# Joint attention stage: the query groups of a head in the order 0, 1, 3, 2

## The reference

```
s = einsum('bqhd,bkhd->bhqk', qb, k) * scale
s = s + cb[..., None] - c[:, :, None, :]
s = where(key_pos[None, :] <= q_pos[:, None], s, -inf)
p = softmax(s, axis=-1)
return einsum('bhqk,bkhd->bqhd', p, v)
```

## Time and profile before

| | us |
|---|---|
| median of 3 runs (lowest to highest) | 3654.77 (3650.62 to 3657.84) |
| the profiled execution | 3655.24 |
| its span, first to last instruction | 3653.5 |
| attention stage, first to last score | 747.4 |

### The profile page before, as it was taken

How to read it: one execution, slowest core, us unless ns; L and a number is a source line. 1 busy time by engine, 2 the same in 40 slices (tenths; PEclk the granted TensorE clock), 3 DMA queues, 4 the chain that set the end, 5 groups by cost and what they waited for, 6 DMA issues and landing times. The chain is left out here.

```text
span 3653.5 us, 48316 instructions
## 1 busy us (share of the span) xinstructions
PE 3245.6 (89%) x18078; PEld 2856.5 (78%) x18078; DVE 2103.9 (58%) x3533; ACT 837.4 (23%) x1492; POOL 491.5 (13%) x277
## 2 busy tenths in 40 slices
PE   5999999828988899956998799999998799999996
PEld 5999999715555555534676799999998699999995
DVE  5001112266666666623433587787786678778776
ACT  5111111213333333312222211111112211111112
POOL 0000000031111111000000422222223122222220
PEclk9999999858988999978999899999999899999997
DMA  4223222133221322163343311111112411111112
GB/s 110 70 70 105 64 61 61 31 88 81 64 62 47 81 56 73 30 203 113 104 137 121 111 46 46 46 46 46 46 46 84 120 46 46 46 46 46 46 46 82
DMA packets 250600, 262.36 MB, mean 72 GB/s; under 512 B 38074, under 2 KB 207435, under 8 KB 244515
## 3 DMA queue, kind: packets, MB, share of 16 engines
q1 hardware_dynamic: 249163, 256.81, 24.5%
q10 hardware_dynamic: 1344, 4.36, 0.6%
HBM read 192.08 MB, written 69.05 MB: 71 GB/s over the span
## 5 line engine op out<-in xcount | busy, mean ns | idle before, releaser
L2155 PE MATMUL ps_ffn<-h,wsp_n 128*128 128x312 f32 (+1 forms) x6336 | 1054.3, 322 | 44.0 <-POOL h L1991 29.9
L2155 PEld LDWEIGHTS ps_ffn<-h,wsp_n 128*128 128x128 f32 x6336 | 1015.1, 189 | 50.3 <-issue 38.8
L2090 DVE TENSOR_TENSOR yacc<-ps_ffn,yacc 128x312 f32<-128x312 f32 (+1 forms) x1056 | 495.1, 515 | 220.5 <-PE ps_ffn L2170 220.5
L391 PE MATMUL ps_project<-hT,wsp 128*128 128x416 f32 x3000 | 579.3, 353 | 3.2 <-DVE wsp L335 3.2
L391 PEld LDWEIGHTS ps_project<-hT,wsp 128*128 128x128 f32 x3000 | 561.3, 188 | 12.0 <-issue 4.9
L2170 PE MATMUL ps_ffn<-aT,dsp 128*128 128x312 f32 (+1 forms) x3168 | 544.9, 321 | 9.8 <-DVE yacc L2090 9.8
L2170 PEld LDWEIGHTS ps_ffn<-aT,dsp 128*128 128x128 f32 x3168 | 508.4, 188 | 12.6 <-issue 9.8
L1986 POOL TENSOR_TENSOR wsp_n<-wraw_n,wsp_n 128x1024 fp32r<-128x1024 f32 x88 | 210.5, 2392 | 801.8 <-ACT wsp_n L2027 801.8
L2104 DVE RECIPROCAL silu<-silu 128x416 f32<-128x416 f32 x132 | 306.2, 2320 | 4.5
L1012 PE MATMUL ps_fox<-pexp,va 128*65 128x512 f32 (+3 forms) x640 | 298.1, 548 | 4.7 <-ACT pexp L1155 4.7
L2057 ACT ACTIVATE aT<-a 128x416 fp32r<-128x416 f32 x132 | 65.2, 494 | 1005.5 <-DVE a L2112 1005.5
(11 more groups left out here) (235 smaller groups left out, 3062.3 us busy)
## 6 DMA issues: line engine op xcount, KB each, us to landing
wraw_n<-in_w_gate_dram SPq DMA_DIRECT2D x44, 512.0 KB, 3.9
wraw_n<-in_w_up_dram SPq DMA_DIRECT2D x44, 512.0 KB, 3.8
draw<-in_w_down_dram SPq DMA_DIRECT2D x44, 512.0 KB, 3.6
qk_raw<-zT SPq DMA_DIRECT2D x32, 512.0 KB
zT<-zs SPq DMA_DIRECT2D x12, 1040.0 KB
wraw<-in_w_in_dram SPq DMA_DIRECT2D x24, 512.0 KB
x<-x2s SPq DMA_DIRECT2D x20, 416.0 KB
h2T<-hT_m SPq DMA_DIRECT2D x20, 416.0 KB
```

The source lines that it names most:

```text
L391: last = pe.matmul(ps[:, g, 0:BLK], wsp[:, b, s, k, :], hT[:, g * TPB:(g + 1) * TPB, v, k, :], start=m == 0, stop=m == 3 * KD - 1)
L2090: dve.tensor_tensor(y, ps[:, 4 + i, 0:FB[b] * TT], y, ALU.add).then_inc(added, 1)
L2155: last = pe.matmul(ps[:, 2 * q + s, 0:FB[b] * TT], wsp[:, par, s, w, k, :], h2[:, FB0[b]:FB0[b + 1], v, k, :], start=m == 0, stop=m == 3 * ...
```

## The change

The order of the groups within each head goes from 0, 1, 2, 3 to 0, 1, 3, 2. Everything that counts by `group(u)`, `blocks(u)` and `runs(u)` follows it.

```
-GORDER = (0, 1, 2, 3)
+GORDER = (0, 1, 3, 2)
```

## The result

| | before | after |
|---|---|---|
| median of 20 runs each, us | 3657.45 (3650.62 to 3663.12) | 3663.47 (3659.57 to 3674.63) |
| profiled execution, us | 3655.24 | 3661.24 |
| attention stage, first score to its last instruction, us | 755.9 | 759.9 |

The ratio is 1.0023 [1.0015, 1.0031]: slower, by 6.0 us between the medians, where 1.7 us faster was forecast. The time lies inside the stated range of 3640 to 3664, near its edge and on the other side of no change. The two profiled executions are 6.0 us apart as well: 4.0 in the attention stage, and 2.0 in the stages around it, which the change doesn't touch (the feed-forward stage alone, first to last instruction, takes between 1645.7 and 1649.8 us in the profiles of this study, in either order). So the 4.0 are to be explained.

What follows compares the result with a forecast made beforehand. Attention stage: TensorE busy 667.2 of 747.4 us, idle mostly waiting for VectorE's maxima. Terms +11.5 - 10.7 - 2.5 = -1.7 us on 3654.8 gave 3653.1 us; own range 3645 to 3660, 8-in-10 range 3640 to 3664.

Steps and rivals of the forecast that it cites:

- ScalarE's copies and GpSimd's work keep their blocks: First units of heads 2 and 3: their long stops, up to 8.1 us, stay; listed under what costs nothing.
- term A: Group 1's units: a fourth maximum in 32 blocks adds 0.36 us wait each, 11.5 us slower; bounds 0 and 19.
- term B: Engine collisions in the two-a-block units of heads 2 to 5: of 21.7 us, 10.7 go; bounds 3 and 18.
- term C: Quiet two-a-block units of heads 1, 6 and 7: 2.5 us of TensorE idle time go; bounds 0 and 4.
- rival 2: Collisions only move: 3 us go in term B, none in term C; +8.5, 3663 us; chance 0.13.
- rival 3: Group 1's units: four maxima a block drop the granted clock to 1.2 GHz; +18, 3673 us; chance 0.09.
- waits for an exp: TensorE waiting for the exp behind ScalarE's copies: 4.7 us grows, so 7.6 us stay in term B.
- the stuck VectorE: Heads 2 to 5: TensorE waits 0 to 1.70 us each for VectorE's late reductions; 0.5 taken, so 2 us stay.
- The half clock: Lowered granted clock in the units of heads 2 to 5: 1.4 us stay; bounds 0 and 8.6.
- The sign that was named for rival 2: Group 3's units over 34 us in heads 2 to 5 would show the forecast wrong.
- head 0, which the sum left out with a remark: Head 0's unit may have another part of the idle time; noted only with the upper bound 4 of term C.
- SyncE's later load: Load of the head after next issued at block 28, not 24; costs nothing, covered by GpSimd's 261.4 us wait.

Runs made afterwards that it cites:

- experiment 1: Changed order plus one wait: GpSimd's cast L944 for the head after head 4 lets VectorE's last query factor finish first; 3658.85 us, ratio 1.0009.
- Experiment 3: Order before, with one maximum moved a block later (last of head 3's four for head 4, block 34 not 33); 3658.84 us, ratio 1.0005.
- experiment 2: Order before plus one wait holding GpSimd's cast L944 at the start of head 4 until VectorE's end factors are done; 3658.81 us, ratio 1.0003.
- experiment 7: The changed order measured again, nothing else altered; 3664.09 us, ratio 1.0016.
- experiments 5: Changed order plus waits holding GpSimd's L944 in five heads and L949 in four until VectorE's end factors are done; 3632.99 us, ratio 0.9944.
- 6: Order before plus waits holding GpSimd's L944 in five heads and L949 in four until VectorE's end factors are done; 3628.66 us, ratio 0.9916.
- experiment 9: Order before, GpSimd's L944 and L949 held for VectorE's end factors, plus two waits for negations at L947 and L949; 3615.09 us, ratio 0.9885.
- 10: Kernel of experiment 9 with group 1's 12 maxima spread over five blocks (3, 2, 3, 2, 2) instead of four; 3606.43 us, ratio 0.9858.

## Why the prediction was wrong

**The step that failed** is the one priced at nothing: "ScalarE's copies and GpSimd's work keep their blocks". GpSimd did keep its place, but VectorE did not keep its own. The last maximum of the head now stands one block later, VectorE came to the last query factor some 0.4 us later after the head's last score (0.71 us after that score's mask L1002 began, before 0.33), and a race won by 0.06 us was lost. This cost 2.0 us at head 3's end and up to 4.3 in head 4's first unit in the profile (2.7 of them went in experiment 1), and 4.6 us of the median by experiment 1. Without it no difference between the two orders can be told (1.0009 and 1.0003): where the forecast stood, but for 1.7 us that cannot be told from none either. Experiment 3 showed that the place of one maximum is enough; that this same shift is what loses the race in the changed order is argued from the two timelines.

The lost race is not the whole of the miss. Between the forecast of -1.7 and the profile's +4.0 lie 5.7 us: -1.9 from term A, +2.1 from term B (the 2.0 at head 3's end), +3.7 from term C, whose sign was wrong, and +1.8 in group 0's units, which the sum left at nothing. Those 1.8 are head 4's +4.3 and head 3's -2.4, and the latter is not the order's doing: in experiment 2, which is the kernel before up to that point, head 3's unit took 20.0 us, and in the profile before 23.1. The measured 3663.5 us is also the number of rival 2, by chance: that rival let only 3 us go in term B, and 8.6 went.

**Term A, +11.5: the mechanism and the price were right, and shown in six of the eight heads.** The fourth maximum waits 0.36 us, in 24 blocks of heads 2 to 7. In heads 0 and 1 the units grew by 1.4 and 1.5 only (in the second profile of the changed order, of experiment 7, by 6.7 and 0.3, so these two settle nothing): in head 0 TensorE stood before too, 2.25 and 2.99 us, for a VectorE that was itself held, and in head 1 the clock is low in both (0.78 in the earlier trace rows, 0.80 after). 9.6 in all. Nothing of rival 3 came: the granted clock of group 1's units in heads 2 to 7 is 1.00.

**Term B, -10.7: right in the sum, and spoilt by the failed step.** -8.6 was measured, and the 2.0 at head 3's end are the new collision; without them it is -10.6. Two of its parts were near: 8.4 us of waits for an exp over six times (7.6 forecast), 6.4 of them in heads 2 to 5, and one wait of 1.7 for the stuck VectorE (2). The forecast had put all four waits for an exp into heads 2 to 5; one of them, 0.64 us, stood in head 0, and head 5 had none. The half clock was mis-sized: all four units are at 0.95, which by the forecast's own measure is up to 0.05 x 139.6 = 7.0 us, where 1.4 were taken. That the sum came out near all the same is in part luck. The sign that was named for rival 2, units over 34 us, was drawn too tight: all four are over 34 (34.5 to 35.5), but 31.4 + 11.0 / 4 is already 34.2.

**Term C, -2.5: wrong sign, +1.2.** Heads 1 and 6 gave 1.1 and 0.6, head 7 lost 0.6, and head 0, which the sum left out with a remark, lost 2.3: its exp behind the copies came 0.7 us later (1.34 in place of 0.64), and a wait of 1.32 us for the laid maxima stood at the end of group 3's unit, where none had been. The copies stand in every head from 0 to 6; I had priced them only where they were long.

**SyncE's later load** cost nothing, as said: GpSimd waits for the last score, 249.0 us, and the one wait for a load, 41.3 us for head 1, is there in both.

**What stays open.** Head 0's unit of group 1 differs between runs of one kernel: 28.1 and 33.4 us in two profiles of the changed order, 26.7 and 30.4 in those of the order before and of experiment 3, which touches only head 4's maxima. GpSimd starts there when a load lands. How much of the medians' 6.0 against the profiles' 4.0 comes from it was not measured. The profile of experiment 7 has 762.9 us for the stage, 7.0 over before, and 6.7 of them are this unit; group 3's unit of head 2 takes 33.0 there and 34.6 in the first. So a table by units from one execution each is good to a few microseconds, and the experiments carry more than it does.

## What to carry to other kernels

When two engines race for a port, an edit that touches neither of them can flip the race: for every such pair in the trace, write down by how much it is won, and price those won by less than the edit shifts. A wait that settles the race for good is nearly free where the engine held back has slack (GpSimd waits 249 us here), and such waits were worth 43 us, against the 4 to 6 that the reordering moved; but each also shifts what comes later, and can bring the next pair together. And count each collision away before an ordering is judged: by itself this order costs 15.7 us, of which 11.7 were hidden because it happened to spare others.

## What was not expected of the hardware

- A VectorE instruction of four numbers a partition was held as long as a large one: L1239, `TENSOR_SCALAR` on 128x4, took 3.69, 3.75, 3.80 and 4.21 us beside GpSimd's 4.5 us subtraction. It takes 0.17 in most places (all 32 in the profile before), and 0.39 to 2.87 in a few others of experiments 5, 6, 9 and 10. The same page and section of the Trainium skill counts this operation among those that can take the shared ports; the trace agrees. Reductions from PSUM are not held: the 36 of L1232 that lie wholly inside a large instruction of GpSimd in the trace before take 0.69 us at most, as do the 280 elsewhere. In experiment 1 the first pair below runs ahead of a subtraction, the second mostly beside it; only their widths differ:
```profile
1226.50 0.89 DVE L1234 TENSOR_REDUCE tops<-ps_fox 128x1 f32<-128x512 f32 x2
...
1227.78 1.02 DVE L1234 TENSOR_REDUCE tops<-ps_fox 128x1 f32<-128x512 f32 x2 [0.40 <-PE ps_fox L972]
1227.91 4.51 POOL L949 TENSOR_TENSOR k_lo_rows<-qk_raw,k_hi_rows 64x2048 fp32r<-64x2048 f32 x1
```
- All collisions between these two engines that the waits of experiment 9 remove cost together 43 us of the order before in the profiles and 43 between the medians, nearly half of it in two units: group 0's of heads 2 and 3 went from 22.6 and 23.1 us to 13.4 and 13.0.
